# Gathering the experts' output rows at the end: four plain loads with VectorE additions, and place matrices built on GpSimd

## The chip, the cores and the metric

The kernel runs on one core of one Trainium2 chip. The metric is the device time of one execution in microseconds (us), the median of three runs.

## The reference, cut to what matters

One layer of an encoder, 512 tokens of 1024 channels: a mixer, then a mixture of 16 experts, then a final norm. Each token takes two experts; each expert is a SwiGLU block of inner width 512. The kernel computes only the token-expert pairs that the routing chose.

```
out = zeros
for e in range(16):
    a = silu(t @ w_gate[e]) * (t @ w_up[e])
    out = out + gate[:, e:e + 1] * (a @ w_down[e])   # gate is zero for 14 of 16 experts of a token
x = x + out
result = rmsnorm(x, norm_final)
```

## The kernel before, in words

**Layout.** Tokens are four blocks of 128 (`TB = 4`). The residual `x2` is [128, 4, 1024] in SBUF. The routing gives each expert a tile of 128 slots, and overflow tiles would follow where an expert has over 128 pairs (with this input none runs).

**Expert loop.** For each expert, SyncE loads six weight chunks of 1 MB into a ring of twelve raw buffers. ScalarE (`split_hi`, L481) rounds a chunk into `ring_hi`, VectorE (`split_lo`, L487) subtracts it from the raw chunk into `ring_lo`, with both inputs in SBUF and 2048 elements a partition. TensorE multiplies three times per product (`three`, L519 to L521). The chunks are numbered: the last expert's down weights are `C_OVER - 2` and `C_OVER - 1`. VectorE's order is written out by hand: with the expert chunks counted from `C_MOE` (0 to 95), its step `NE - 3` ends with chunk 92, chunk 93, `gated`, `place_tile` twice, chunk 94, `aT_l`, chunk 95.

**Output of the first fourteen experts.** GpSimd scatters each tile of 128 scaled rows into the DRAM tensor `y_rows` by an indirect DMA (`y_store`, L793). Row 2k+r of `y_rows` belongs to token k's expert of rank r; unused rows are zero, written early from `zero_rows`. When all fourteen stores have landed (`y_out`), GpSimd issues eight accumulating DMAs (L830): for r = 0 and then r = 1, for each block t, `x2[:, t, :] += rows_of(t, r)`. The second one for a block waits for the first (`y_back`).

**Output of the last two experts.** Their rows stay on chip. `yl_high` (ScalarE, L1113) and `yl_low` (VectorE, L2277) scale and split them. TensorE adds them to the right tokens by multiplying with a place matrix (`placed`, L1714 and L1716), 128x128 zeros and ones per expert and block. VectorE's `place_tile` (L2262 to L2270) builds the eight matrices: one copy of the row numbers, three subtractions on one column, four comparisons, for each of two experts.

**End.** VectorE's `add_placed` (L2283, L2287) waits for `y_back[t]` and for TensorE's sum, and adds the sum to `x2`. ScalarE squares it (L1182), GpSimd takes the inverse root (L842, L844), VectorE scales (L2363) and SyncE stores `out`.

**Memory.** The place matrices lie where raw buffer 7 lies, free once chunk 91 (`C_OVER - 5`) is split. `raw_a` is raw buffers 0 to 2.

Of the kernel before, what the change touches and what calls it, by code (L numbers as in the profile page):

```python
# [24 lines left out]
ALU = mybir.AluOpType  # L25
# [3 lines left out]
P = 128  # L29
# [5 lines left out]
D = 1024  # L35
# [60 lines left out]
def build_trunk(nc, x, mem, norm_mix, norm_mem, w_in, w_pool, pool_scale, w_kv_mem, w_up_sb,  # L96
# [9 lines left out]
    def sb(name, shape, dt, region, offset=None):  # L106
        size = 1
        for n in shape[1:]:
            size *= n
        size *= 2 if dt == BF16 else 4  # L110
        if offset is None:
            offset = cursor.get(region, 0)
            cursor[region] = offset + (size + 31) // 32 * 32
        return nc.alloc_sbuf_tensor_at(name, shape, dt, offset=at[region] + offset)
# [155 lines left out]
    tok = [sb(f"tok{i}", [P, TB], F32, "m", 62 * KB + 32 * i) for i in range(2)]  # L270
    place_l = [sb(f"place_l{i}", [P, TB, P], F32R, "t", 2 * i * KB) for i in range(2)]
    gfin_bc = sb("gfin_bc", [P, D], F32, "t", 24 * KB)
    LAST = 2
    junk3 = sb("junk3", [P, D], F32, "m", 64 * KB)

# [21 lines left out]
    with ctx:  # L297
        sems = {}

        def sem(name):  # L300
            sems[name] = ctx.enter_context(nc.semaphore(name))
            return sems[name]
# [112 lines left out]
        y_out = [sem("y_out0"), sem("y_out1")]  # L415
        ye_free = sem("ye_free")
        y_zero = sem("y_zero")
        zero_set = sem("zero_set")
        wts_ready = sem("wts_ready")
        w_split = sem("w_split")  # L420
        at_w_ready = sem("at_w_ready")
        w_ps = sem("w_ps")
        w_ready = sem("w_ready")
# [66 lines left out]
        def K(c0, i=None, per=0):  # L490
            return (c0, i, per)
# [12 lines left out]
        def rows_of(t, r):  # L504
            return y_rows[2 * t * P:2 * (t + 1) * P, :].rearrange("(p r) d -> p r d", r=2)[:, r, :]
# [19 lines left out]
        def _(sp):  # L525
# [121 lines left out]
            for i in range(2):  # L647
                c = K(C_OVER - 2 + i)
                raw_free(c)
                expert_out(c, i, NE - 1)  # L650

            n_over = sp.value_load(tab[0:1, 0:1], min_val=0, max_val=OVER)
            with sp.If(n_over > 0):
                with sp.Fori(0, OVER) as j:
                    with sp.If(n_over > j):
                        e = sp.value_load(tab[0:1, bass.ds(j + 1, 1)], min_val=0, max_val=NE - 1)
                        for i in range(4):
                            c = K(C_OVER + i, j, PER_E)
                            sp.wait_ge(lo_ready, split_count(c, RAW_OVER))
                            expert_in(c, i, e)  # L660
                        for i in range(2):
                            c = K(C_OVER + 4 + i, j, PER_E)
                            sp.wait_ge(lo_ready, split_count(c, RAW_OVER))
                            expert_out(c, i, e)
                    sp.nop()
                sp.wait_ge(over_done, 1)
# [12 lines left out]
        def _(pool):  # L679
# [57 lines left out]
                           allow_small_or_imprecise_dtypes=True))  # L737
            pool.sem_inc(consts_ready, 1)
            pool.sem_inc(ye_free, 2)
            pool.memset(zero_rows[:, :], 0.0).then_inc(zero_set, 1)  # L740
            inverse_root(slice(TB, TB + MB), TB + MB)
            for g in range(4):
                lo = DH * (g % 2)
# [3 lines left out]
            pool.dma_start(bias_bc[:, 0:NG], b_group[0:1, :].broadcast_to([P, NG])).then_inc(small_in, 16)  # L747
            pool.dma_start(bias_bc[:, NG:NG + NE], b_router[0:1, :].broadcast_to([P, NE])).then_inc(small_in, 16)
            pool.wait_ge(lo_ready, C_PAIR[0] + 1)
            pool.wait_ge(zero_set, 1)  # L750
            for c in range(2 * TB):
                pool.dma_start(y_rows[c * P:(c + 1) * P, :], zero_rows[:, :]).then_inc(y_zero, 16)
            pool.wait_ge(av_ps, HEADS)
# [28 lines left out]
            def y_store(tile, b, earlier):  # L782

                pool.tensor_copy(y_col[b][:, :], y_row[:, bass.ds(tile, 1)]).then_inc(y_col_set, 1)
                pool.wait_ge(y_col_set, tile + 1)
                pool.sem_inc(pool_free, 1)
                if earlier is not None:
                    pool.wait_ge(y_out[1 - b], 16 * earlier)
                    pool.sem_inc(ye_free, 1)
                pool.wait_ge(y_a, tile + 1)  # L790
                pool.wait_ge(y_v, tile + 1)
                pool.sem_inc(pool_free, 1)
                pool.indirect_dma_start(y_rows[:, :], bass.IndirectOffsetOnAxis(y_col[b][:, :].bitcast(U32), 0),  # L793
                                        ye[b][:, :], None, bounds_check=2 * S - 1, oob_is_err=False).then_inc(y_out[b], 16)
# [5 lines left out]

            w_all = wts[:, :, :].rearrange("p r t -> p (r t)")
            pool.wait_ge(wts_ready, 1)
            pool.tensor_copy(w_parts[:, :, 0], w_all).then_inc(w_split, 1)
            pool.wait_ge(w_split, 1)
            pool.tensor_tensor(w_rest[:, :], w_all, w_parts[:, :, 0], ALU.subtract).then_inc(w_split, 1)
            pool.wait_ge(w_split, 2)
            pool.tensor_copy(w_parts[:, :, 1], w_rest[:, :]).then_inc(w_split, 1)
            pool.wait_ge(w_split, 3)
            pool.tensor_tensor(w_parts[:, :, 2], w_rest[:, :], w_parts[:, :, 1], ALU.subtract).then_inc(w_split, 1)
            pool.wait_ge(w_split, 4)  # L810
            pool.tensor_tensor(at_w[:, :, :, :],
                               at_tile[:, :, :].unsqueeze(2).broadcast_to([P, 2 * TB, 3, SLOT_TILES]),
                               w_parts[:, :, :].unsqueeze(3).broadcast_to([P, 2 * TB, 3, SLOT_TILES]),
# [3 lines left out]
            with pool.Fori(0, NE // 2 - 2) as j:  # L817
                for n in range(2):
                    step = pool.snap(j * 2 + n)
                    x_load(step + 4, n, step + 3)  # L820
                    y_store(step + 1, (n + 1) % 2, j + 1)
            y_store(NE - 3, 1, NE // 2 - 1)
            for b in range(2):
                pool.wait_ge(y_out[b], 16 * (NE // 2 - 1))
                pool.sem_inc(pool_free, 1)
            for r in range(2):
                for t in range(TB):
                    if r == 1:
                        pool.wait_ge(y_back[t], 16)
                    pool.dma_start(x2[:, t, :], rows_of(t, r), accum_op=ALU.add).then_inc(y_back[t], 16)  # L830
            pool.wait_ge(route_ready, 1)
            n_over = pool.value_load(tab[0:1, 0:1], min_val=0, max_val=OVER)
            with pool.If(n_over > 0):
# [916 lines left out]
        def _(dve):  # L1750
# [509 lines left out]
            def place_tile(b, tile, n):  # L2260

                dve.tensor_copy(tok[b][:, 0:1], x_row[:, bass.ds(tile, 1)]).then_inc(tok_set, 1)  # L2262
                dve.wait_ge(tok_set, 2 * n + 1)
                for t in range(1, TB):
                    ins = dve.tensor_scalar(tok[b][:, t:t + 1], tok[b][:, 0:1], float(-P * t), None, ALU.add)
                ins.then_inc(tok_set, 1)
                dve.wait_ge(tok_set, 2 * n + 2)
                for t in range(TB):
                    dve.tensor_scalar(place_l[b][:, t, :], slot_no_f[:, :], tok[b][:, t:t + 1], None,
                                      ALU.is_equal).then_inc(place_set, 1)  # L2270

            def yl_low(b, n, tile, yb=(5, 6)):

                for half in range(2):
                    part = slice(512 * half, 512 * half + 512)
                    dve.wait_ge(yl_h, n + half)
                    dve.scalar_tensor_tensor(yl_lo[b][:, part], bank(yb[half]), w_slot[:, bass.ds(tile, 1)],  # L2277
                                             yl_hi[b][:, part].bitcast(F32), ALU.mult, ALU.subtract).then_inc(yl_l, 1)
# [36 lines left out]
            for step in (NE - 4, NE - 3):  # L2315
                c0 = C_MOE + 10 + PER_E * step
                for i in range(PER_E):
                    if step == NE - 3 and i == PER_E - 1:
                        aT_l(NE, aT_lo_end, aT_hi_end)
                    split_lo(dve, K(c0 + i + 2))  # L2320
                    if i == 0:
                        y_half(K(c0 - 1), step % 2, step)
                    if i == 1:
                        aT_l(step + 2)
                    if i == 3:
                        gated(step + 3)
                        if step == NE - 4:
                            xe_lo(NE)
                        else:
                            place_tile(0, NE - 2, 0)  # L2330
                            place_tile(1, NE - 1, 1)
            yl_low(0, 1, NE - 2)
            yl_low(1, 3, NE - 1, END_BANK)
            dve.wait_ge(gfin_in, 16)
            for t in range(TB):
                dve.wait_ge(y_back[t], 32)
                add_placed(t, t + 1)
            n_over = dve.value_load(tab[0:1, 0:1], min_val=0, max_val=OVER)
            with dve.If(n_over > 0):
                with dve.Fori(0, OVER) as j:  # L2340
                    with dve.If(n_over > j):
                        xe_lo(j + NE + 1)
                        for i in range(PER_E):
                            split_lo(dve, K(C_OVER + i, j, PER_E))
                        gated(j + NE + 1)
                        aT_l(j + NE + 1)
                        dve.wait_ge(place_set, 2 * TB + TB * j)
                        place_tile(0, j + NE, j + 2)
                        yl_low(0, 2 * j + 2 * LAST + 1, j + NE)
                        for t in range(TB):  # L2350
                            add_placed(t, TB * j + TB + t + 1)
                        dve.wait_ge(sum_done, TB * j + 2 * TB)
                        dve.sem_inc(over_added, 1)
                    dve.nop()
                dve.sem_inc(over_done, 1)
# [31 lines left out]
```

## Time and profile before

| what | us |
|---|---|
| median of 3 runs (lowest, highest) | 730.58 (729.27, 730.77) |
| the profiled execution's own time | 730.31 |
| its span | 728.6 |
| TensorE busy (share of the span) | 699.1 (96%) |
| VectorE busy | 518.7 (71%) |
| ScalarE busy | 401.8 (55%) |
| GpSimd busy | 128.5 (18%) |

The trace counts from the span's start. A row of a timeline gives the start, the duration of the group, the engine (PE is TensorE, DVE is VectorE, ACT is ScalarE, POOL is GpSimd), the line, the instruction, what it writes and reads, how many there are, and in brackets the idle time before it with what ended that.

### The profile page before, as it was taken

Reading aid. Unit: us, or ns where it says so; the run is one execution under the profiler, and the core shown is the slowest. Engines: PE = TensorE matmul, PEld = TensorE weight load, DVE = VectorE, ACT = ScalarE, POOL = GpSimd, SP = SyncE. Lnnn points to the kernel's source line nnn. Section 1 sums busy time; section 2 is a strip of 40 time slices with the busy share of each in tenths; the row PEclk is TensorE's granted clock in tenths of the full one; section 3 lists DMA queues with packets and bytes.
Section 4 is the critical chain, followed back from the end, with each engine's and each line's share of the span. In section 5 each row is a group of like instructions: output and inputs, shape, how many; then the busy total and the mean of one; then the engine's idle time right before and its main releaser. Section 6 shows DMA issues by size and latency. Waiting matters only on the chain.

```text
span 728.6 us, 9970 instructions
## 1 busy us (share of the span) xinstructions
PE 699.1 (96%) x3557; PEld 582.1 (80%) x3557; DVE 518.7 (71%) x554; ACT 401.8 (55%) x407; POOL 128.5 (18%) x145
## 2 busy tenths in 40 slices
PE   5999999999999999999999989999999999999982
PEld 4898888888888888888889758888888888888861
DVE  4688776898526061441744678999999999999975
ACT  6626665666522131222403336877777777777742
POOL 5320000000000000000000150333333333333132
PEclk9999999999999999999999999999999999999997
DMA  9675330000232233223593379999999999999886
GB/s 327 165 263 180 116 97 20 29 13 4 94 124 80 92 101 121 95 87 113 177 363 126 130 269 393 395 390 369 372 365 379 373 369 371 373 368 372 316 159 188
DMA packets 86753, 159.15 MB, mean 218 GB/s; under 512 B 6274, under 2 KB 37116, under 8 KB 86724
## 3 DMA queue, kind: packets, MB, share of 16 engines
q1 hardware_dynamic: 78544, 137.38, 53.0%
q0 software_dynamic: 8128, 21.37, 9.3%
q8 instruction: 19, 0.31, 0.2%
q14 instruction: 10, 0.08, 0.0%
q10 hardware_dynamic: 52, 0.01, 0.0%
HBM read 150.64 MB, written 15.73 MB: 228 GB/s over the span
## 4 chain that ended last, share of the span: by engine, by line
PE 84%; DVE 5%; DMA 5%; ACT 3%; issue 1%; POOL 1%; POOLq 0%; SPq 0%; DVEq 0%; ACTq 0%
PE ps L519 24%; PE ps L521 24%; PE ps L520 24%; DMA x<-y_rows 3%; PE ps L1614 2%; DVE ring_lo L487 2%; PE ps L1540 1%; DMA xn<-in_x 1%; PE ps L1671 1%; PE ps L1568 1%; PE ps L1398 1%; DVE soft L1935 1%; PE ps L1360 1%; PE ps L1640 1%; ACT ring_hi L481 1%
## 5 line engine op out<-in xcount | busy, mean ns | idle before, releaser
L487 DVE TENSOR_TENSOR ring_lo<-raw_a,ring_hi 128x2048 fp32r<-128x2048 f32 (+2 forms) x58 | 115.5, 1995 | 96.7 <-ACT ring_hi L481 96.7
L487 DVE TENSOR_TENSOR ring_lo<-raw,ring_hi 128x2048 fp32r<-128x2048 f32 x71 | 161.3, 2290 | 11.1 <-ACT ring_hi L481 9.9
L481 ACT ACTIVATE ring_hi<-raw 128x2048 fp32r<-128x2048 f32 x71 | 136.2, 1920 | 19.3 <-PE ps L521 19.3
L481 ACT ACTIVATE ring_hi<-raw_a 128x2048 fp32r<-128x2048 f32 (+2 forms) x58 | 97.4, 1680 | 33.5 <-PE ps L521 30.6
L519 PE MATMUL ps<-hT_hi,ring_hi 128*128 128x512 f32 x288 | 113.4, 394 | 1.6 <-DVE hT_lo L1791 1.0
L521 PE MATMUL ps<-hT_hi,ring_lo 128*128 128x512 f32 x288 | 112.2, 390 | 0.0
L520 PE MATMUL ps<-hT_lo,ring_hi 128*128 128x512 f32 x288 | 112.2, 390 | 0.0
L519 PE MATMUL ps<-ring_hi,xT_hi 128*128 128x512 f32 x240 | 95.0, 396 | 1.8 <-DVE xT_lo L2173 1.7
L521 PE MATMUL ps<-ring_hi,xT_lo 128*128 128x512 f32 x240 | 93.8, 391 | 0.0
L520 PE MATMUL ps<-ring_lo,xT_hi 128*128 128x512 f32 x240 | 93.6, 390 | 0.0
L519 PEld LDWEIGHTS ps<-hT_hi,ring_hi 128*128 128x128 f32 x288 | 54.1, 188 | 13.0 <-DVE ring_lo L1786 1.2
L521 PEld LDWEIGHTS ps<-hT_hi,ring_lo 128*128 128x128 f32 x288 | 54.1, 188 | 11.4
L520 PEld LDWEIGHTS ps<-hT_lo,ring_hi 128*128 128x128 f32 x288 | 54.1, 188 | 10.7
L793 POOL DMA_INDIRECT y_rows<-ye,y_col x14 | 31.0, 2212 | 161.7 <-DVE ye L2258 161.7
L519 PEld LDWEIGHTS ps<-ring_hi,xT_hi 128*128 128x128 f32 x240 | 45.1, 188 | 11.5 <-DVE xT_lo L2173 2.0
L1051 ACT ACTIVATE sig<-ps 128x1024 f32<-128x1024 f32 x12 | 12.3, 1027 | 74.2 <-PE ps L521 74.2
L521 PEld LDWEIGHTS ps<-ring_hi,xT_lo 128*128 128x128 f32 x240 | 45.0, 188 | 9.5
L520 PEld LDWEIGHTS ps<-ring_lo,xT_hi 128*128 128x128 f32 x240 | 45.1, 188 | 9.0
L519 PE MATMUL ps<-ring_hi,aT_hi 128*128 128x512 f32 x120 | 48.1, 401 | 0.0
L521 PE MATMUL ps<-ring_hi,aT_lo 128*128 128x512 f32 x120 | 47.0, 392 | 0.0
L520 PE MATMUL ps<-ring_lo,aT_hi 128*128 128x512 f32 x120 | 46.9, 391 | 0.0
L778 POOL DMA_INDIRECT xe<-h_rows,x_col x15 | 34.2, 2282 | 12.9 <-POOL x_col L775 12.9
(369 smaller groups left out, 1241.1 us busy)
## 6 DMA issues: line engine op xcount, KB each, us to landing
raw<-in_w_down SPq DMA_DIRECT2D x25, 1024.0 KB
raw<-in_w_gate SPq DMA_DIRECT2D x47, 512.0 KB
raw<-in_w_up SPq DMA_DIRECT2D x47, 512.0 KB
raw_a<-in_w_in SPq DMA_DIRECT2D x15, 1024.0 KB
raw_a<-in_w_gate SPq DMA_DIRECT2D x17, 512.0 KB
raw_a<-in_w_up SPq DMA_DIRECT2D x17, 512.0 KB
raw_a<-in_w_down SPq DMA_DIRECT2D x7, 1024.0 KB
raw_a<-in_w_in SPq DMA_DIRECT2D x10, 512.0 KB, 8.3
```

What stands on the lines that cost most here:

```text
L481: act.activation(ring_hi[:, c[0] % SPLIT, 0:width], buf[:, 0:width], ACT.Copy).then_inc(hi_ready, 1)
L487: dve.tensor_tensor(ring_lo[:, s, 0:width], buf[:, 0:width], ring_hi[:, s, 0:width].bitcast(F32), ALU.subtract).then_inc(lo_ready, 1)
L519: pe.matmul(out_ap, l_hi, r_hi, start=start, stop=False, skip_group_check=True)
L520: pe.matmul(out_ap, l_hi, r_lo, start=False, stop=False, skip_group_check=True)
L521: return pe.matmul(out_ap, l_lo, r_hi, start=False, stop=stop, skip_group_check=True)
L778: pool.indirect_dma_start(xe[b][:, :], None, h2_rows[:, :], bass.IndirectOffsetOnAxis(x_col[b][:, :].bitcast(U32), 0), bounds_check=S - 1, ...
L793: pool.indirect_dma_start(y_rows[:, :], bass.IndirectOffsetOnAxis(y_col[b][:, :].bitcast(U32), 0), ye[b][:, :], None, bounds_check=2 * S - ...
L1051: act.activation(sig[:, i, :, :], gate_pair(i), ACT.Sigmoid).then_inc(g_sig, 1)
L1360: pe.matmul(zz[:, o:o + w], lhs[:, :], soft_hi[:, j:j + w], start=False, stop=False, skip_group_check=True)
L1398: ins = pe.matmul(bank(3 * h, 3)[:, o:o + w], kx[rows, p % 2, keys], qx[rows, p % 2, sbk * P:], start=False, stop=end, skip_group_check=True)
L1540: ins = pe.matmul(bank(LG[t])[:, o:o + NG + NE], x2T[:, t, k, :], wr[:, k, :], start=k == 0, stop=k == KD - 1)
L1614: ins = pe.transpose(bank(2, 2)[:, k * P:(k + 1) * P], xe[b][:, k * P:(k + 1) * P], ident[:, :])
```

## The change

SyncE gets four plain loads of the r = 0 rows into `y_in`, a view of `raw_a`, after it has waited for the fourteen stores. GpSimd issues only the four accumulating DMAs of r = 1. VectorE adds `y_in` to `x2` (`add_rows`): blocks 0 and 1 between its two `yl_low`, block 2 after them, block 3 between the sums of blocks 1 and 2. `place_tile` for the last two experts is taken from VectorE; GpSimd does the same sixteen small instructions, with a wait after each dependent group, between its last `y_store` and its wait for the stores. Two semaphores of GpSimd (`zero_set`, `w_split`) are replaced by its own counting semaphore.

```diff
--- before.py
+++ after.py
@@ -270,6 +270,7 @@
     tok = [sb(f"tok{i}", [P, TB], F32, "m", 62 * KB + 32 * i) for i in range(2)]
     place_l = [sb(f"place_l{i}", [P, TB, P], F32R, "t", 2 * i * KB) for i in range(2)]
     gfin_bc = sb("gfin_bc", [P, D], F32, "t", 24 * KB)
+    y_in = raw_a[:, :, :].rearrange("p s (h d) -> p (s h) d", d=D)
     LAST = 2
     junk3 = sb("junk3", [P, D], F32, "m", 64 * KB)
 
@@ -415,9 +416,9 @@
         y_out = [sem("y_out0"), sem("y_out1")]
         ye_free = sem("ye_free")
         y_zero = sem("y_zero")
-        zero_set = sem("zero_set")
+        y_load = [sem(f"y_load{b}") for b in range(2)]
+        y_added = sem("y_added")
         wts_ready = sem("wts_ready")
-        w_split = sem("w_split")
         at_w_ready = sem("at_w_ready")
         w_ps = sem("w_ps")
         w_ready = sem("w_ready")
@@ -649,8 +650,16 @@
                 raw_free(c)
                 expert_out(c, i, NE - 1)
 
+            sp.wait_ge(lo_ready, split_count(K(C_OVER - 11)))
+            for b in range(2):
+                sp.wait_ge(y_out[b], 16 * (NE // 2 - 1))
+                sp.sem_inc(sp_free, 1)
+            for t in range(TB):
+                sp.dma_start(y_in[:, t, :], rows_of(t, 0)).then_inc(y_load[t // 2], 16)
             n_over = sp.value_load(tab[0:1, 0:1], min_val=0, max_val=OVER)
             with sp.If(n_over > 0):
+                sp.wait_ge(y_added, TB)
+                sp.sem_inc(sp_free, 1)
                 with sp.Fori(0, OVER) as j:
                     with sp.If(n_over > j):
                         e = sp.value_load(tab[0:1, bass.ds(j + 1, 1)], min_val=0, max_val=NE - 1)
@@ -737,7 +746,7 @@
                            allow_small_or_imprecise_dtypes=True))
             pool.sem_inc(consts_ready, 1)
             pool.sem_inc(ye_free, 2)
-            pool.memset(zero_rows[:, :], 0.0).then_inc(zero_set, 1)
+            step(pool.memset(zero_rows[:, :], 0.0))
             inverse_root(slice(TB, TB + MB), TB + MB)
             for g in range(4):
                 lo = DH * (g % 2)
@@ -747,7 +756,6 @@
             pool.dma_start(bias_bc[:, 0:NG], b_group[0:1, :].broadcast_to([P, NG])).then_inc(small_in, 16)
             pool.dma_start(bias_bc[:, NG:NG + NE], b_router[0:1, :].broadcast_to([P, NE])).then_inc(small_in, 16)
             pool.wait_ge(lo_ready, C_PAIR[0] + 1)
-            pool.wait_ge(zero_set, 1)
             for c in range(2 * TB):
                 pool.dma_start(y_rows[c * P:(c + 1) * P, :], zero_rows[:, :]).then_inc(y_zero, 16)
             pool.wait_ge(av_ps, HEADS)
@@ -800,14 +808,11 @@
 
             w_all = wts[:, :, :].rearrange("p r t -> p (r t)")
             pool.wait_ge(wts_ready, 1)
-            pool.tensor_copy(w_parts[:, :, 0], w_all).then_inc(w_split, 1)
-            pool.wait_ge(w_split, 1)
-            pool.tensor_tensor(w_rest[:, :], w_all, w_parts[:, :, 0], ALU.subtract).then_inc(w_split, 1)
-            pool.wait_ge(w_split, 2)
-            pool.tensor_copy(w_parts[:, :, 1], w_rest[:, :]).then_inc(w_split, 1)
-            pool.wait_ge(w_split, 3)
-            pool.tensor_tensor(w_parts[:, :, 2], w_rest[:, :], w_parts[:, :, 1], ALU.subtract).then_inc(w_split, 1)
-            pool.wait_ge(w_split, 4)
+            done = step
+            step(pool.tensor_copy(w_parts[:, :, 0], w_all))
+            step(pool.tensor_tensor(w_rest[:, :], w_all, w_parts[:, :, 0], ALU.subtract))
+            step(pool.tensor_copy(w_parts[:, :, 1], w_rest[:, :]))
+            step(pool.tensor_tensor(w_parts[:, :, 2], w_rest[:, :], w_parts[:, :, 1], ALU.subtract))
             pool.tensor_tensor(at_w[:, :, :, :],
                                at_tile[:, :, :].unsqueeze(2).broadcast_to([P, 2 * TB, 3, SLOT_TILES]),
                                w_parts[:, :, :].unsqueeze(3).broadcast_to([P, 2 * TB, 3, SLOT_TILES]),
@@ -820,14 +825,20 @@
                     x_load(step + 4, n, step + 3)
                     y_store(step + 1, (n + 1) % 2, j + 1)
             y_store(NE - 3, 1, NE // 2 - 1)
+            pool.wait_ge(lo_ready, split_count(K(C_OVER - 5)))
+            for b, tile in ((0, NE - 2), (1, NE - 1)):
+                done(pool.tensor_copy(tok[b][:, 0:1], x_row[:, tile:tile + 1]))
+                for t in range(1, TB):
+                    ins = pool.tensor_scalar(tok[b][:, t:t + 1], tok[b][:, 0:1], float(-P * t), None, ALU.add)
+                done(ins)
+                for t in range(TB):
+                    pool.tensor_scalar(place_l[b][:, t, :], slot_no_f[:, :], tok[b][:, t:t + 1], None,
+                                       ALU.is_equal).then_inc(place_set, 1)
             for b in range(2):
                 pool.wait_ge(y_out[b], 16 * (NE // 2 - 1))
                 pool.sem_inc(pool_free, 1)
-            for r in range(2):
-                for t in range(TB):
-                    if r == 1:
-                        pool.wait_ge(y_back[t], 16)
-                    pool.dma_start(x2[:, t, :], rows_of(t, r), accum_op=ALU.add).then_inc(y_back[t], 16)
+            for t in range(TB):
+                pool.dma_start(x2[:, t, :], rows_of(t, 1), accum_op=ALU.add).then_inc(y_back[t], 16)
             pool.wait_ge(route_ready, 1)
             n_over = pool.value_load(tab[0:1, 0:1], min_val=0, max_val=OVER)
             with pool.If(n_over > 0):
@@ -2326,14 +2337,21 @@
                         gated(step + 3)
                         if step == NE - 4:
                             xe_lo(NE)
-                        else:
-                            place_tile(0, NE - 2, 0)
-                            place_tile(1, NE - 1, 1)
+            def add_rows(t):
+                dve.wait_ge(y_load[t // 2], 32)
+                dve.wait_ge(y_back[t], 16)
+                dve.tensor_tensor(x2[:, t, :], x2[:, t, :], y_in[:, t, :], ALU.add).then_inc(y_added, 1)
+
             yl_low(0, 1, NE - 2)
+            add_rows(0)
+            add_rows(1)
             yl_low(1, 3, NE - 1, END_BANK)
+            add_rows(2)
             dve.wait_ge(gfin_in, 16)
             for t in range(TB):
-                dve.wait_ge(y_back[t], 32)
+                if t == 2:
+                    add_rows(3)
+                dve.wait_ge(y_added, min(t + 1 + t // 2, TB))
                 add_placed(t, t + 1)
             n_over = dve.value_load(tab[0:1, 0:1], min_val=0, max_val=OVER)
             with dve.If(n_over > 0):
@@ -2345,7 +2363,7 @@
                         gated(j + NE + 1)
                         aT_l(j + NE + 1)
                         dve.wait_ge(place_set, 2 * TB + TB * j)
-                        place_tile(0, j + NE, j + 2)
+                        place_tile(0, j + NE, j)
                         yl_low(0, 2 * j + 2 * LAST + 1, j + NE)
                         for t in range(TB):
                             add_placed(t, TB * j + TB + t + 1)
```

## Rows read from the trace of the kernel before

**Rows 1.** Chain of waits, 676 to 729 us, its shares by line.

```profile
by line: DMA x<-y_rows 38.8%; issue 10.8%; DMA y_rows<-ye,y_col 10.0%; POOL x L830 3.9%; ACT ring_hi L481 3.6%; PE ps L521 3.5%; PE ps L520 3.5%; PE ps L519 3.4%; POOLq L297 2.9%; DVE x L2287 2.4%; POOL ms L842 2.2%; ACT junk L1182 2.0%; DV
```

**Rows 2.** Timeline of POOL, 655 to 729 us (start us, us, engine, line, instruction).

```profile
693.51 3.71 POOL L830 DMA_DIRECT2D x<-y_rows  x4 [3.68 <-DMA y_rows<-ye,y_col]
699.34 0.86 POOL L830 DMA_DIRECT2D x<-y_rows  x1 [2.12 <-DMA x<-y_rows]
702.68 0.86 POOL L830 DMA_DIRECT2D x<-y_rows  x1 [2.48 <-DMA x<-y_rows]
705.17 0.86 POOL L830 DMA_DIRECT2D x<-y_rows  x1 [1.63 <-DMA x<-y_rows]
707.65 0.86 POOL L830 DMA_DIRECT2D x<-y_rows  x1 [1.62 <-DMA x<-y_rows]
...
720.59 1.17 POOL L842 TENSOR_SCALAR ms<-ss 128x1 f32<-128x1 f32 x1 [2.42 <-ACT junk L1182]
```

**Rows 3.** Timeline of DVE, 655 to 729 us.

```profile
690.13 4.63 DVE L487 TENSOR_TENSOR ring_lo<-raw,ring_hi 128x2048 fp32r<-128x2048 f32 x2 [0.56 <-ACT ring_hi L481]
...
695.76 0.87 DVE L2269 TENSOR_SCALAR place_l<-slot_no_f,tok 128x128 fp32r<-128x128 f32 x4
...
697.84 2.28 DVE L487 TENSOR_TENSOR ring_lo<-raw,ring_hi 128x2048 fp32r<-128x2048 f32 x1
...
707.32 1.41 DVE L2277 SCALAR_TENSOR_TENSOR yl_lo<-ps,w_slot,yl_hi 128x512 fp32r<-128x512 f32 x2 [3.08 <-ACT yl_hi L1113]
710.11 1.23 DVE L2283 TENSOR_TENSOR x<-ps,x 128x1024 f32<-128x1024 f32 x1 [1.38 <-PE ps L1716]
...
718.04 1.29 DVE L2287 TENSOR_TENSOR x<-ps,x 128x512 f32<-128x512 f32 x2 [1.95 <-DMA x<-y_rows]
719.24 3.67 DVE L2363 SCALAR_TENSOR_TENSOR x<-x,rstd,gfin_bc 128x1024 f32<-128x1024 f32 x3
```

**Rows 4.** Timeline of ACT, 655 to 729 us.

```profile
693.67 1.91 ACT L481 ACTIVATE ring_hi<-raw 128x2048 fp32r<-128x2048 f32 x1
...
696.83 1.91 ACT L481 ACTIVATE ring_hi<-raw 128x2048 fp32r<-128x2048 f32 x1
```

**Rows 5.** Timeline of PE, 696 to 729 us.

```profile
706.39 0.39 PE L1714 MATMUL ps<-yl_hi,place_l 128*128 128x512 f32 x1
...
708.78 0.50 PE L1714 MATMUL ps<-yl_hi,place_l 128*128 128x512 f32 x1 [0.41 <-DVE yl_lo L2277]
...
714.13 0.39 PE L1716 MATMUL ps<-yl_lo,place_l 128*128 128x512 f32 x1
```

**Rows 6.** Stretches by window: PE, PEld, DVE, ACT, POOL busy, clock, DMA share, GB/s.

```profile
704.00:706.00 2.00, 2.00 (x11) 1.65 (x10) 0.24 (x1) 0.00 (x0) 0.83 (x1) 1.00 1.06 209
...
722.00:724.00 2.00, 0.00 (x0) 0.00 (x0) 1.56 (x2) 0.00 (x0) 1.31 (x1) 0.50 1.01 399
```

**Rows 7.** Groups of POOL by form (busy us, mean ns of one).

```profile
L784 POOL COPY y_col<-y_row 128x1 int32 x12 | 15.6, 1300 | 0.0
...
L775 POOL COPY x_col<-x_row 128x1 int32<-128x1 int32 x3 | 0.6, 187 | 6.6 <-DVE x_row L2218 5.3 <-PE ps L1614 1.3
...
L701 POOL TENSOR_SCALAR_AFFINE_SELECT tri_f<-tri_f 128x128 f32<-128x128 f32 x1 | 0.3, 297 | 0.1
```

**Rows 8.** Timeline of DVE, then of POOL, 420 to 470 us.

```profile
462.24 2.29 DVE L487 TENSOR_TENSOR ring_lo<-raw,ring_hi 128x2048 fp32r<-128x2048 f32 x1
...
460.45 1.91 POOL L775 COPY x_col<-x_row 128x1 int32 x1
```

**Rows 9.** PE by window (its busy time, clock, DMA share, GB/s) and its timeline.

```profile
717.50:718.00 0.50, 0.00 (x0) 0.66 0.00 0
...
399.00:400.00 1.00, 1.00 (x4) 0.50 0.00 0
...
398.83 0.63 PE L520 MATMUL ps<-ring_lo,mgT_hi 128*128 128x512 f32 x1
399.25 0.63 PE L521 MATMUL ps<-ring_hi,mgT_lo 128*128 128x512 f32 x1
```

## The prediction, made before the changed kernel was run

> **What bounds the kernel now.** I read the chain of waits first, for the last 53 us: the DMAs that bring `y_rows` back into `x2` hold 38.8% of it [rows 1]. Up to there the chain is TensorE's products, which the change leaves alone. Then GpSimd's timeline: the first four accumulating DMAs are issued from 693.51 us, when the last store has landed; the second four go out at 699.34, 702.68, 705.17 and 707.65, each when its block's first has landed [rows 2]. Seen from the first issue, four accumulates land after 5.8, 9.2, 11.7 and 14.1 us. VectorE adds the last block at 718.04 because the eighth landed only then, and is done at S = 718.04 + 1.29 = 719.33 [rows 3]. The other operand was there earlier: TensorE's last place product starts at 714.13 [rows 5]. The DMA engines were at a share of 1.06 while they moved 209 GB/s in accumulates, and at 1.01 with 399 GB/s in plain stores [rows 6], so an accumulate costs them twice a plain DMA. From S to the end of the span are 9.3 us of norm and store. I write the result as a shift of S.
>
> **The change, part by part.** F is the time at which GpSimd issues its first accumulate, 693.51 before.
>
> *Four plain loads for four accumulates.* SyncE has issued its weights and is idle; it starts at about 693.0, on the same stores. Four loads of 512 KB at 399 GB/s take 5.3 us plus about 1.5 us of start (taken from the accumulates, issued at 693.51 and at 209 GB/s 2.5 us apart, of which the first needs 5.8), so they are there at about 700, if nothing shares the engines. The last accumulate lands at F + 14.1 in place of 718.0. With F unchanged that would be 3 to 10 us sooner, which is the change's offer.
>
> *VectorE's additions.* Four of 128x1024 with both inputs in SBUF: half of a split of 2048, 2.28 us [rows 3], so 1.15 us each. `add_rows(1)` stands ahead of the second `yl_low`, and waits for the second accumulate. So everything behind it on VectorE, the low half of the last expert's rows first, waits until F + 9.2 + 1.15, and TensorE's last 24 products wait for that. Before, this `yl_low` ran at 707.32 [rows 3].
>
> *Place matrices off VectorE.* It did them between `gated` and chunk 94, which began at 697.84 though ScalarE had its high half at 693.67 + 1.91 = 695.6 [rows 3, 4]. Chunk 94 now starts at 695.6, chunk 95 when its high half is ready, 696.83 + 1.91 = 698.75. TensorE's last expert ends up to 1.9 us sooner (706.39 less 1.9 = 704.5) [rows 5]. It is worth something only if nothing else is later.
>
> *Place matrices on GpSimd.* This is the term that decides. They stand between the last `y_store`, over at 693.51 - 3.68 = 689.83 [rows 2], and the accumulates. Alone they are cheap: the tiny ones 0.187 us each; a comparison of 128x128 is taken as the 128x128 select, 0.297 us [rows 7]. The trace has no comparison of this form on GpSimd; I bound it by 0.19 (the 128x1 copy) and 0.6. Twice (4 x 0.19 + 4 x 0.30) and about 0.08 for each of four waits is 4.2 us, so F would be about 694.6. But GpSimd is not alone. The same 128x1 copy takes 1.3 us on average in the expert loop [rows 7]. One instance: a copy started at 460.45 and ended at 462.36, just after VectorE's next split began at 462.24 [rows 8]; another: 1.17 us for L842 from 720.59, while VectorE scales `x2` [rows 2, 3]. So a GpSimd instruction that reads SBUF waits for VectorE's running instruction with two SBUF inputs, and one gets through as VectorE goes from one to the next. VectorE has two splits from 690.13 to 694.76, one from 695.6 to 697.9, one from 698.75 to 701.05. I walk GpSimd through them, one instruction per boundary: the copy at 689.85; the three subtractions at 690.1, 692.4 and 694.8; comparisons 1 and 2 by 695.7; comparisons 3 and 4 and the second tile's copy between 697.9 and 698.7; three subtractions and four comparisons from 701.05 to 702.9. The issue follows after the 0.6 us that it took before (692.9, the landing, to 693.51). F = 703.5. TensorE's first place product is not before 704.5, so the matrices are in time; only the accumulates are late.
>
> *The chain from F.* The loads are long there. The second accumulate lands at 712.7; `add_rows(1)` ends at 713.8; `yl_low` of the last expert, 1.41 us, at 715.2, where it was 708.73. `add_rows(2)`, sums 0 and 1, `add_rows(3)` (its accumulate lands at 717.6) and sum 2 fill VectorE to about 721.4 (1.15 and 1.15 us, and 1.23 for each sum [rows 3]). TensorE's 24 products took from 708.78 to 714.13 and 0.39 [rows 5], 5.7 us: its last sum would be there at 720.9. But TensorE has idled since 706.3 by then. After its last product in this trace the granted clock is at 0.66 between 717.5 and 718.0, falling to the lower level, some 3 us idle [rows 5, 9]. At that level, 1.2 GHz, products follow each other by 0.42 us (398.83 to 399.25) [rows 9], against 0.23 at 2.4 GHz (5.35 us over 23 steps [rows 5]). Bounds are none of the 24 slow (0) and all (4.6 us). I take eight, 1.5 us, since the slow stretch around 399 was a short one of a few us. The last sum is ready at 722.4, added by 723.8. S moves from 719.3 to 723.8, 4.5 us.
>
> *The rest.* The two semaphores replaced cost nothing: `zero_rows` is cleared long before VectorE or the DMAs need it, and the weight split has expert 0's down product for cover; without it each wait would cost about 0.1 us. The norm and the stores keep their 9.3 us. SyncE's wait delays only the stores of `out`, which come after.
>
> **Sum.** Against the profiled execution's 730.31: minus 1.9 on TensorE and the earlier end of the accumulates, both swallowed; plus 4.5 on S. 734.8 us. The median of the runs shown, 730.58, is 0.3 above the profiled execution, which I leave out.
>
> **The rivals.** *(A) GpSimd gets through quickly, faster.* The place is the stretch from 689.8 to 694.6; if comparisons pass beside VectorE's splits, F is 694.6. Loads and accumulates then share engines that are full [rows 6]: 5.3 us of plain work and 4 x 2.6 of accumulates, 16 us, end at about 711.5, and VectorE's tail from the third block (1.15, 1.23, 1.23, 1.15, 1.23, 1.29, 7.3 us) ends at 717.5 to 718. GpSimd's inverse roots then meet VectorE's scaling more closely, up to 0.8 more. The result is 728.6 to 729.1. It decides at F = 699.5: from there S is at 719.3 again (20.3 us from F with the slow products, 19 without). For it: the select's 0.297 us. Against it: the 1300 ns copies [rows 7].
>
> *(B) GpSimd holds VectorE.* Instructions that stand ready without a wait between them might pass in one block, and VectorE's split waits. A wait stands between copy, subtractions and comparisons, and each lets a split in. Then the three subtractions go at 692.4, four comparisons and a copy at 695.2, and chunk 94 starts at 696.5 in place of 695.6; three subtractions at 698.7, four comparisons at 699.4, chunk 95 at 700.6, where it was before. F is 701.2, S 721.5, the time 732.5. The Trainium skill, "SBUF — State Buffer", section "Who interferes with whom", says that whichever of the two issues first gets the shared pair for the whole instruction and the other fully blocks. By that rule GpSimd can block VectorE as well. The trace shows only the blocked GpSimd.
>
> *(C) TensorE stays at the lower clock for all 24 products.* S is 3.1 us later than forecast, 737.9. For it: it has idled 9 us. Against: the clock came back within a few us at 399 [rows 9].
>
> **How the numbers follow.** The forecast, 734.8, has 0.54; A 0.2, B 0.18, C 0.08. About 0.2% (1.5 us) is what a measurement of this kernel can tell from no change. A is faster with 0.16 and within the bound with 0.04; B's lower edge and a comparison much cheaper than I take put another 0.08 within it; the rest, 0.72, is slower. Since these cases have both signs, the forecast's own range is 733 to 737 (comparisons of 0.19 to 0.6 us move F by less than 1.5 either way, the slow products by -1.5 to +1). The whole range, which reaches into A and to near C, is 728.9 to 737.
>
> **What would show it.** In the profile after: L830 is issued first at about 703.5, not 694.6; the comparisons on GpSimd have some of over 1 us, each ending just after a split of VectorE; chunk 94 starts at 695.6; `add_rows(1)` waits for the accumulate, idle by about 9 us in all; `yl_low` of the last expert ends near 715; TensorE's clock is at half for some of the last products. If the comparisons end by 695 the forecast is wrong and A holds; if VectorE's splits start late with GpSimd busy, B.

## The result, and the profile after

The changed kernel takes 736.83 us, median of four runs (736.50 to 737.84), against 730.61 us before. The ratio is 1.0089, interval 1.0077 to 1.0101: it is slower. The profiled execution is the slowest of the four, 737.84 us with a span of 735.7; before it was 730.31 with 728.6. Of the difference of the two, 0.6 us is there already when GpSimd issues its last `y_store` (688.23 against 687.64 us): it is scatter of executions, ahead of anything that changed. 7.5 us less these is 6.9, and so much is looked for at the end. Line numbers after are about 11 higher: L487 is L488, `place_tile`'s comparison on GpSimd is L835, its subtractions L832, the accumulating DMAs L841, `add_rows` L2343, the sums L2294 and L2298, the place products L1725 and L1727.

The chain of waits of the changed kernel, its last 60 us, by line. It answers to [rows 1]:

```profile
by line: DMA x<-y_rows 14.2%; POOL place_l L835 13.7%; POOL tok L832 9.1%; issue 7.7%; PE ps L1725 7.2%; PE ps L1727 6.6%; POOL y_rows L801 3.7%; ACT ring_hi L482 3.2%; PE ps L522 3.1%; PE ps L521 3.1%; PE ps L520 3.0%; POOLq L298 2.5%; DVE
```

The DMAs are a smaller part than before. In their place stand GpSimd's comparisons and, of all things, its subtractions on one column, 22.8% together.

The timeline of GpSimd after, then the same asked for in narrow windows, so that single instructions show:

```profile
690.72 4.86 POOL L832 TENSOR_SCALAR tok<-tok 128x1 f32<-128x1 f32 x3
695.67 6.44 POOL L835 TENSOR_SCALAR place_l<-slot_no_f,tok 128x128 fp32r<-128x128 f32 x4
...
702.34 0.56 POOL L832 TENSOR_SCALAR tok<-tok 128x1 f32<-128x1 f32 x3
703.00 2.37 POOL L835 TENSOR_SCALAR place_l<-slot_no_f,tok 128x128 fp32r<-128x128 f32 x4
705.33 3.68 POOL L841 DMA_DIRECT2D x<-y_rows  x4
...
690.72 2.38 POOL L832 TENSOR_SCALAR tok<-tok 128x1 f32<-128x1 f32 x1
...
693.07 2.33 POOL L832 TENSOR_SCALAR tok<-tok 128x1 f32<-128x1 f32 x1
...
696.28 2.68 POOL L835 TENSOR_SCALAR place_l<-slot_no_f,tok 128x128 fp32r<-128x128 f32 x1
...
699.52 2.59 POOL L835 TENSOR_SCALAR place_l<-slot_no_f,tok 128x128 fp32r<-128x128 f32 x1
...
704.78 0.59 POOL L835 TENSOR_SCALAR place_l<-slot_no_f,tok 128x128 fp32r<-128x128 f32 x1
```

The timeline of VectorE after; it answers to [rows 3]:

```profile
690.71 4.64 DVE L488 TENSOR_TENSOR ring_lo<-raw,ring_hi 128x2048 fp32r<-128x2048 f32 x2 [0.55 <-ACT ring_hi L482]
...
696.19 2.29 DVE L488 TENSOR_TENSOR ring_lo<-raw,ring_hi 128x2048 fp32r<-128x2048 f32 x1 [0.25 <-ACT ring_hi L482]
...
699.36 2.29 DVE L488 TENSOR_TENSOR ring_lo<-raw,ring_hi 128x2048 fp32r<-128x2048 f32 x1 [0.27 <-ACT ring_hi L482]
...
710.96 1.23 DVE L2343 TENSOR_TENSOR x<-x,raw_a 128x1024 f32<-128x1024 f32 x1 [7.99 <-DMA x<-y_rows]
714.61 1.23 DVE L2343 TENSOR_TENSOR x<-x,raw_a 128x1024 f32<-128x1024 f32 x1 [2.42 <-DMA x<-y_rows]
715.75 1.41 DVE L2288 SCALAR_TENSOR_TENSOR yl_lo<-ps,w_slot,yl_hi 128x512 fp32r<-128x512 f32 x2
...
725.56 1.29 DVE L2298 TENSOR_TENSOR x<-ps,x 128x512 f32<-128x512 f32 x2 [0.59 <-PE ps L1727]
```

Lay the two timelines side by side. VectorE's two splits run from 690.71 to 695.35. A subtraction on a column of 128 values, 0.19 us by itself, starts at 690.72 and takes 2.38 us; the next one takes 2.33 us, to 695.40. The comparison from 696.28 takes 2.68 us and ends 0.48 us after the split that began at 696.19; the one from 699.52 takes 2.59 us and ends 0.46 us after the split that began at 699.36. That split is over at 701.65, and up to 710.96 VectorE has no instruction with two SBUF inputs: the three subtractions of the second tile now take 0.56 us together and its four comparisons 2.37 us, also while `yl_low`, with one input in PSUM, still runs. So the accumulates are issued at 705.33, where the last store had let them go at about 693.5. VectorE waits 7.99 us for the first block, then 2.42 for the second, and `yl_low` is done at 717.16.

The timeline of TensorE after, then its windows (PE busy, granted clock, DMA share, GB/s). They answer to [rows 5, 9]:

```profile
717.21 0.80 PE L1725 MATMUL ps<-yl_hi,place_l 128*128 128x512 f32 x1 [9.66 <-DVE yl_lo L2288]
717.80 0.63 PE L1727 MATMUL ps<-yl_lo,place_l 128*128 128x512 f32 x1
718.22 0.63 PE L1725 MATMUL ps<-yl_hi,place_l 128*128 128x512 f32 x1
...
722.49 0.46 PE L1725 MATMUL ps<-yl_hi,place_l 128*128 128x512 f32 x1
722.79 0.40 PE L1727 MATMUL ps<-yl_lo,place_l 128*128 128x512 f32 x1
...
716.00:717.00 1.00, 0.00 (x0) 0.50 1.09 213
...
722.00:723.00 1.00, 1.00 (x4) 0.70 0.00 0
```

TensorE had idled 9.66 us. The clock was at 0.50, the level of 1.2 GHz; twelve products follow each other by 0.43 us (the first by 0.59), the other twelve by 0.23. VectorE's last sum waits for them (0.59 us in its row) and ends at S = 726.86, against 719.33.

### The profile page after: what moved, and what is told of

The parts are those of the page before. It is cut to its first block, busy times and chain, and to the rows that moved or that the text cites. A ratio compares the mean times of both kernels' runs of the same rounds, so it can differ in the third digit from the quotient of the medians.

```text
span 735.7 us, 9980 instructions
## 1 busy us (share of the span) xinstructions
PE 701.9 (95%) x3557; PEld 584.4 (79%) x3557; DVE 520.9 (71%) x542; ACT 401.6 (55%) x407; POOL 139.2 (19%) x157
## 4 chain that ended last, share of the span: by engine, by line
PE 85%; DVE 6%; ACT 3%; POOL 2%; DMA 2%; issue 1%; POOLq 0%; ACTq 0%; DVEq 0%
PE ps L520 24%; PE ps L522 24%; PE ps L521 24%; PE ps L1625 2%; DVE ring_lo L488 2%; DMA x<-y_rows 1%; POOL place_l L835 1%; PE ps L1682 1%; PE ps L1551 1%; PE ps L1579 1%; PE ps L1409 1%; DVE soft L1946 1%; PE ps L1371 1%; PE ps L1651 1%; ACT ring_hi L482 1%
## 5 line engine op out<-in xcount | busy, mean ns | idle before, releaser
L488 DVE TENSOR_TENSOR ring_lo<-raw_a,ring_hi 128x2048 fp32r<-128x2048 f32 (+2 forms) x58 | 115.5, 1994 | 96.7 <-ACT ring_hi L482 96.7
L488 DVE TENSOR_TENSOR ring_lo<-raw,ring_hi 128x2048 fp32r<-128x2048 f32 x71 | 161.3, 2289 | 11.7 <-ACT ring_hi L482 10.4
```

The source lines that it names most:

```text
L488: dve.tensor_tensor(ring_lo[:, s, 0:width], buf[:, 0:width], ring_hi[:, s, 0:width].bitcast(F32), ALU.subtract).then_inc(lo_ready, 1)
```

## The experiments

Theory 1 is that of the prediction: GpSimd's place matrices wait for VectorE's splits and delay the accumulates, and the rest follows. Theory 2 puts the loss on the other half of the change, the loads and the additions, which share the DMA engines and stand ahead of the last `yl_low`.

### Each half alone

The first run, e1_place_dve, is the changed kernel with the place matrices back on VectorE.

```diff
-            pool.wait_ge(lo_ready, split_count(K(C_OVER - 5)))
-            for b, tile in ((0, NE - 2), (1, NE - 1)):
...
+                        else:
+                            place_tile(0, NE - 2, 0)
+                            place_tile(1, NE - 1, 1)
```

> The place matrices go back to VectorE, all else as changed. Theory 1 (GpSimd's comparisons wait for VectorE's splits and so delay the accumulates): the first accumulate is issued at about 694 instead of 705.3 us, and the time is 728.5 to 730. Theory 2 (the loss is the plain loads and the additions: they share the DMA engines and stand ahead of the last yl_low): the time stays at 735 to 737.

Measured: 729.52 us, ratio to before 0.9981 (0.9967 to 0.9994), first accumulate at 694.17. The loads and additions alone are a small gain, 0.2%.

The second, e2_place_pool_only, is the kernel before with GpSimd's block of the change ahead of its eight accumulates.

```diff
             y_store(NE - 3, 1, NE // 2 - 1)
+            pool.wait_ge(lo_ready, split_count(K(C_OVER - 5)))
+            for b, tile in ((0, NE - 2), (1, NE - 1)):
...
-                        else:
-                            place_tile(0, NE - 2, 0)
-                            place_tile(1, NE - 1, 1)
```

> The kernel before with one part of the change alone: GpSimd builds the place matrices ahead of its eight accumulating DMAs. Theory 1: first accumulate at about 705, the eighth lands 24.5 us later, the additions end at about 731 instead of 719.3, and the time is 741 to 743. Theory 2 (only loads and additions cost): 729 to 731.

Measured: 742.52 us, ratio 1.0161 (1.0130 to 1.0193). GpSimd's timeline, then VectorE's last sum, in this run:

```profile
694.86 6.44 POOL L831 TENSOR_SCALAR place_l<-slot_no_f,tok 128x128 fp32r<-128x128 f32 x4
...
704.51 3.67 POOL L840 DMA_DIRECT2D x<-y_rows  x4
...
719.20 0.86 POOL L840 DMA_DIRECT2D x<-y_rows  x1 [1.62 <-DMA x<-y_rows]
...
728.88 1.29 DVE L2297 TENSOR_TENSOR x<-ps,x 128x512 f32<-128x512 f32 x2 [1.25 <-DMA x<-y_rows]
```

The delay of 11 us goes through undamped: the place matrices alone cost 11.8 us. In the whole change the loads halve the number of accumulates behind them, and that brings the loss down to 6.2 us. Theory 2 has no place for either run.

### The same work elsewhere in GpSimd's order

In e3_issue_first the four accumulating DMAs of the changed kernel, and GpSimd's wait for the stores, come ahead of the place matrices.

```diff
             y_store(NE - 3, 1, NE // 2 - 1)
-            pool.wait_ge(lo_ready, split_count(K(C_OVER - 5)))
-            for b, tile in ((0, NE - 2), (1, NE - 1)):
...
             for t in range(TB):
                 pool.dma_start(x2[:, t, :], rows_of(t, 1), accum_op=ALU.add).then_inc(y_back[t], 16)
+            pool.wait_ge(lo_ready, split_count(K(C_OVER - 5)))
+            for b, tile in ((0, NE - 2), (1, NE - 1)):
...
```

> As changed, but GpSimd issues its four accumulates first and builds the place matrices after them. Theory 1: accumulates from about 694; the comparisons end at about 704 to 706, at or just after the time TensorE wants them (704.9); the time is 728 to 730. Theory 2: 735 to 737.

Measured: 729.94 us, ratio 0.9989 (0.9977 to 1.0002). GpSimd in this run:

```profile
694.23 3.70 POOL L832 DMA_DIRECT2D x<-y_rows  x4 [3.40 <-DMA y_rows<-ye,y_col]
...
705.11 3.17 POOL L840 TENSOR_SCALAR place_l<-slot_no_f,tok 128x128 fp32r<-128x128 f32 x4
```

The comparisons now end at 708.28, later than I gave them, and TensorE's first place product waits for them (708.34). The second tile's four took 3.17 us, not 2.37: `add_rows(0)`, with two SBUF inputs, ran from 705.43 to 706.66 beside them. TensorE had idled for 2.85 us, and here too its clock fell for a while (granted clock 0.50 between 710 and 712). Still the 7 us are back. What cost was not the work itself but what it stood in front of.

In e7_early the block stands before the expert loop, and its matrices in memory that is long free.

```diff
-    tok = [sb(f"tok{i}", [P, TB], F32, "m", 62 * KB + 32 * i) for i in range(2)]
-    place_l = [sb(f"place_l{i}", [P, TB, P], F32R, "t", 2 * i * KB) for i in range(2)]
+    tok = [oh0, sm[2]]
+    place_l = [sb("place_l0", [P, TB, P], F32R, "t", 28 * KB), sb("place_l1", [P, TB, P], F32R, "const", 512)]
...
                                ALU.mult).then_inc(at_w_ready, 1)
+            for b, tile in ((0, NE - 2), (1, NE - 1)):
...
```

> As changed, but GpSimd builds the place matrices before the expert loop, when it is idle, in memory of the mixer's constants. Theory (the loss is only where the matrices stand): first accumulate at 694.3, chunk 94 at 695.9, time 728 to 729.5. Rival (plain loads and additions cost as well): over 731.

Measured: 730.14 us, ratio 0.9989 (0.9976 to 1.0002), so 0.6 above what I expected and below the rival's 731. The first accumulate is at 693.78, earlier by 0.5, and chunk 94 at 695.94. The block is held by VectorE's splits there as well and takes 15.9 us (437.48 to 453.36), but the `y_store` behind it still waits 5.09 us for VectorE. What I had left out: TensorE ends sooner and then waits longer for `yl_low` behind `add_rows(1)`. Its timeline and windows:

```profile
710.46 0.50 PE L1724 MATMUL ps<-yl_hi,place_l 128*128 128x512 f32 x1 [3.81 <-DVE yl_lo L2287]
...
711.00:712.00 1.00, 1.00 (x4) 0.50 0.67 131
```

The clock falls just as it starts again, and the sums are late (0.73, 0.45 and 0.39 us of waits on VectorE).

### The clock and VectorE's order, with the accumulates late

Both start from the changed kernel. e4_ylow_first moves one of VectorE's steps; e5_keep_clock gives TensorE products to repeat while it waits.

```diff
             yl_low(0, 1, NE - 2)
+            yl_low(1, 3, NE - 1, END_BANK)
             add_rows(0)
             add_rows(1)
-            yl_low(1, 3, NE - 1, END_BANK)
             add_rows(2)
```

> As changed, but VectorE makes the low half of the last expert's rows before add_rows(0) and add_rows(1). The accumulates stay late (705.3). Theory 1: TensorE's 24 products run at full clock before 713, the last accumulate lands at 719.4 and three additions follow: the additions end at about 723.3 instead of 726.9, the time is 733 to 734. Theory 2 (the order alone is the loss): 729 to 731.

```diff
             placed(0, 1, True, False)
+            for _ in range(10):
+                placed(0, 1, True, False)
             pe.wait_ge(yl_l, 4)
```

> As changed, with 40 further place products of TensorE (the second block's first half, again with the same result) in the time in which it waits for the last yl_low. If the lower clock is what sets the end once the accumulates are late: the 24 last products take 5.7 us instead of 8.3, VectorE ends its additions at about 724.5 instead of 726.9, and the time falls by as much as in the run with yl_low first, 0.7 to 1.5 us, to 735.3 to 736.2. If VectorE's order is what cost there: no change, 736.8.

Measured: 736.16 us for the first (ratio 1.0067, 1.0045 to 1.0089), 735.78 for the second (1.0066, 1.0049 to 1.0083). The second is within its expectation, the first is not. Both intervals overlap that of the changed kernel (1.0077 to 1.0101), so what the two edits gave is read from the traces. With the clock kept, the 24 products run at the full rate and S falls, as with the other order. From the issue of the accumulates to S there are 21.5 us in the changed kernel (705.33 to 726.86), 19.5 in e4 (705.05 to 724.57) and 19.7 in e5 (704.05 to 723.78). So the slow products cost about 2 us of S, and both runs take just these away: the order of `yl_low` mattered by way of TensorE. What I got wrong for e4 is the rest. Its VectorE and GpSimd at the end:

```profile
718.62 2.35 DVE L2294 TENSOR_TENSOR x<-ps,x 128x1024 f32<-128x1024 f32 x2
720.89 1.22 DVE L2343 TENSOR_TENSOR x<-x,raw_a 128x1024 f32<-128x1024 f32 x1
722.14 1.23 DVE L2294 TENSOR_TENSOR x<-ps,x 128x1024 f32<-128x1024 f32 x1
...
724.63 1.17 POOL L853 TENSOR_SCALAR ms<-ss 128x1 f32<-128x1 f32 x1 [0.90 <-ACT junk L1193]
725.89 1.47 POOL L855 TENSOR_TENSOR rstd<-ms,neg_half 128x1 f32<-128x1 f32 x1
727.44 1.28 POOL L853 TENSOR_SCALAR ms<-ss 128x1 f32<-128x1 f32 x1
...
729.39 1.41 DVE L2381 SCALAR_TENSOR_TENSOR x<-x,rstd,gfin_bc 128x512 f32<-128x512 f32 x2 [0.72 <-POOL rstd L855]
```

`add_rows(3)` has its rows at about 719.4, but two sums stand ahead of it, so S is 724.6 and not 723.3. Then three of GpSimd's small instructions are held by VectorE's scaling (`x2` and the gains, two SBUF inputs), not two as before, and the last scaling starts 4.8 us after S (724.57), where it was 4.0. The same wait as in the expert loop, once more, takes back 0.8 of the 2 us, and does so in e5 as well (4.8 us from S to the last scaling). I had given it to rival A and forgotten it here.

### VectorE's order, with the accumulates early

e6_dve_order is e1_place_dve and e8_early_order is e7_early, both with this edit:

```diff
             yl_low(0, 1, NE - 2)
-            add_rows(0)
-            add_rows(1)
             yl_low(1, 3, NE - 1, END_BANK)
-            add_rows(2)
...
             for t in range(TB):
-                if t == 2:
-                    add_rows(3)
-                dve.wait_ge(y_added, min(t + 1 + t // 2, TB))
+                add_rows(t)
+                dve.wait_ge(y_added, t + 1)
                 add_placed(t, t + 1)
```

> Place matrices on VectorE, and VectorE's order at the end changed: both yl_low first, then block by block the addition of the loaded rows and of the sum. Theory (with the accumulates early, the order is what is late): additions end at about 716 instead of 718, time 727 to 728.5 against 729.5 of the run without the new order. Rival (the engines' 16 us of DMA work set the end): no change, 729.5.

> Early place matrices on GpSimd and the new VectorE order together. TensorE's sums are then ready by 712.5, the last accumulate lands at about 712 to 713, two additions follow: additions end at about 715.5, time 726.5 to 727.5. If DMA work shared by loads and accumulates ends later than 713: 728 to 729.

Measured: e6 729.51 us, ratio 0.9979 (0.9964 to 0.9994), no gain over e1's 0.9981; e8 727.70 us (727.27 to 728.62), ratio 0.9954 (0.9938 to 0.9971), the fastest kernel here. Its interval lies clear of e7's and just touches those of e1 and e6. The rival for e6 had the right number and the wrong cause: its DMA work does not set the end, VectorE waits for no accumulate there. VectorE in e8, then its windows (busy, clock, DMA share, GB/s):

```profile
705.18 1.41 DVE L2287 SCALAR_TENSOR_TENSOR yl_lo<-ps,w_slot,yl_hi 128x512 fp32r<-128x512 f32 x2 [2.88 <-ACT yl_hi L1123]
706.50 1.21 DVE L2342 TENSOR_TENSOR x<-x,raw_a 128x1024 f32<-128x1024 f32 x1
...
715.12 1.29 DVE L2297 TENSOR_TENSOR x<-ps,x 128x512 f32<-128x512 f32 x2
...
711.00:713.00 2.00, 1.97 (x3) 1.00 0.11 21
```

The DMA engines are through at about 711; VectorE does eight additions in a row from 706.50 to 716.41, with no wait over 0.25 us. In e6 the row of eight starts at 710.96, 4.5 us later. Of these, 2.4 us are scatter: the profiled execution of e6 took 731.63 us, 2.1 above its median, and its last `y_store` is issued at 690.00, against 687.56 in e8. The other 2 us are the place matrices on VectorE's path ahead of the last expert. That they use up what the new order gives is argued from this, not shown by a run. Now VectorE is the bound of the end.

### GpSimd's matrices early, nothing else

```diff
# e9_before_early is the kernel before with the place matrices of e7_early
```

> The kernel before with its eight accumulates, and the place matrices built by GpSimd before the expert loop, so that VectorE is free of them and nothing delays the accumulates. Theory (TensorE and VectorE end up to 1.9 us sooner, but the eighth accumulate sets the end): first accumulate at 693.5, additions end at 719.3, no change, 730 to 731.5. Rival (VectorE's freed 2 us are worth something by themselves): 728.7 to 729.5.

Measured: 730.84 us, ratio 1.0004 (0.9994 to 1.0013), no change. VectorE's last `yl_low` starts at 705.72 instead of 707.32, and its first sum then waits 3.42 us for an accumulate. The 1.9 us on TensorE, which the prediction called swallowed, are swallowed.

## Why the prediction was right or wrong

**The mechanism held, its size did not.** Slower was forecast, by 4.5 us against the profiled execution; the medians differ by 6.2. The ratio of 1.0089 on the 730.58 us that were known is 737.1 us, just past the upper edge of 737. The walk "one instruction per boundary" is what the trace shows: subtractions of 2.38 and 2.33 us, the third at the end of the second split, the last four comparisons after VectorE's last split. Chunk 94 started at 696.19, which is 695.6 without the 0.6 of scatter, as forecast. e1, e2, e3 and e7 show that the late accumulates alone make the loss. The loads were there in time (6.1 us from issue to landing in the median; the 1.5 us of start that I had put in does not follow from the numbers beside it, but nothing hung on it), and the landings followed the issue by 5.6 and 9.3 us (forecast 5.8 and 9.2).

**The step that failed is the size of one term, the comparison on GpSimd.** I took 0.297 us, from the 128x128 select [rows 7], between 0.19 and 0.6; alone it takes 0.59. In the walk this matters twice: in the gap before the split at 696.19 one comparison was done and a second caught, where I had put two done, and in the gap before 699.36 one and not two with the next tile's copy. So the fourth comparison and the second tile's copy were still to do when the last split ended, and the four comparisons after it took 2.37 us and not 1.2. Less the 0.6 of scatter, GpSimd was through at 704.7, and I had 702.9: 1.8 us.

A second error hid a third of that. I had put 0.6 us between the comparisons and the first accumulate, as it took before from the landing to the issue. In the changed kernel the stores had landed long before, and the accumulate is issued at 705.33, as the last comparison ends (704.78 + 0.59 = 705.37). So F is 704.7 for 703.5 forecast, 1.2 us. I also said that a comparison of 0.6 us would move F by less than 1.5; that F came out within this is luck, since by my own walk it moves by 1.8. I placed my value near the low end because the select was the nearest row in shape. The comparison differs from it in more than one way, it reads a scalar per partition from SBUF and writes another type; which of these costs the time was not tried.

**The second term that was too small is the slow products.** I took eight of the 24; twelve were slow, and the first took 0.80 us for 0.50. From the end of `yl_low` to S there are 9.7 us for 8.6 forecast, 1.1 more. The additions show 1.23 us, but the next instruction starts 1.14 after one (714.61 to 715.75), so their 1.15 was right as a step. With 0.1 for the second accumulate, which landed 9.3 us after the issue for 9.2, 4.5 + 1.2 + 1.1 + 0.1 is the 6.9 that the trace has.

**The rivals.** A did not happen here, but e1, e3 and e7 have its early accumulates: 729.5 to 730.1, where it said 728.6 to 729.1, so it put the gain 0.4 to 1.5 us too high. e1's additions end at 716.68 + 1.28 = 717.96, inside the 717.5 to 718 that A gave; its profiled execution is 0.8 us late at the last `y_store` (688.45 against 687.64).

B, in which GpSimd delays chunks 94 and 95 by 0.9 us and more, did not happen: both splits start 0.03 to 0.04 us after their high half and take 2.29 us, the one at 699.36 while a comparison was running (698.95 to 699.55). Its mechanism exists all the same, on a smaller scale. In e7 the same comparisons stand beside splits of the first experts that the changed kernel runs with GpSimd idle. First e7, then the same two splits in the changed kernel:

```profile
441.02 0.61 POOL L826 TENSOR_SCALAR place_l<-slot_no_f,oh 128x128 fp32r<-128x128 f32 x1
441.17 2.37 DVE L488 TENSOR_TENSOR ring_lo<-raw,ring_hi 128x2048 fp32r<-128x2048 f32 x1 [0.69 <-ACT ring_hi L482]
447.88 2.53 POOL L826 TENSOR_SCALAR place_l<-slot_no_f,sm 128x128 fp32r<-128x128 f32 x1
449.88 2.42 DVE L488 TENSOR_TENSOR ring_lo<-raw,ring_hi 128x2048 fp32r<-128x2048 f32 x1
...
441.50 2.29 DVE L488 TENSOR_TENSOR ring_lo<-raw,ring_hi 128x2048 fp32r<-128x2048 f32 x1 [0.69 <-ACT ring_hi L482]
450.22 2.29 DVE L488 TENSOR_TENSOR ring_lo<-raw,ring_hi 128x2048 fp32r<-128x2048 f32 x1
```

The splits take 0.08 and 0.13 us more, where the comparison still had 0.46 and 0.53 us to run. The split between them (443.52) has 0.49 us of overlap and takes 0.11 more. Where the overlap is 0.27 us or less (447.64, and 699.36 in the changed kernel), nothing is added. e9 has the same three longer splits (2.37, 2.40 and 2.42 us).

C, all 24 slow, was half true.

**Left open.** That the wait is for the second SBUF input is shown by coincidence in many rows: GpSimd is held beside splits, `add_rows` and the scaling, and is not held beside VectorE's instructions with one input in PSUM (`yl_low` and the sums). A split with one input was not tried.

## What to carry to other kernels

Before work goes to an idle engine, look at what stands behind it in that engine's queue, and at what its neighbour runs at the time: here sixteen small instructions, some 6.6 us by themselves (an estimate: eight of 0.59, eight of 0.19, four waits of 0.08), took 15 and stood in front of the DMAs that set the end. The same work issued after the DMAs, or in an idle stretch 240 us earlier, cost nothing that the times show. An engine order written out by hand has to be redone when one of its waits moves: the early matrices gave nothing clear in the order of the change (e7, ratio 0.9989, up to 1.0002) and 0.46% with the new one (e8).

## What the runs showed of the hardware

The contention goes both ways, but not evenly. A GpSimd instruction that reads SBUF was held for up to 2.2 us by one of VectorE's splits (0.19 us became 2.38), and got through one at a time, as VectorE went from one split to the next. A split was held by a running comparison for 0.08 to 0.13 us at most (e7 and e9). The Trainium skill, "SBUF — State Buffer", section "Who interferes with whom", has the one that issues first block the other fully. The trace agrees that either side can be held. It does not agree if "first" is read from the start times of the rows: in e3 a GpSimd copy starts at 696.52, 0.08 us ahead of the split at 696.60, and still takes 2.41 us, while the split takes its usual 2.29.

A comparison of 128x128 with a scalar per partition takes GpSimd 0.59 us, twice the select of that shape (0.297 us [rows 7]). Four of them take GpSimd 2.37 us and VectorE 0.87 [rows 3].

TensorE's clock fell with an idle stretch of 9.66 us (changed kernel), with one of 3.81 (e7) and with one of 2.85 (e3); in the last two it fell only after the products had started again. Twelve of the 24 last products ran at 1.2 GHz in the first case, eight in the second. With an idle stretch of 1.53 us it stayed at 1.00 (e1). Forty products that compute nothing new kept it up in e5 (clock 0.994 over the span, 0.986 in the changed kernel) and cost nothing: they ended at 715.3, before `yl_low` at 715.9.
